# Stick-breaking attention on TensorE: the turns of the weight blocks made by the two row halves of the array, in pairs of key blocks, with the scores between both pairs

## The chip, the cores and the metric

One core of one Trainium2 chip runs the whole program. The metric is the device time of one execution in microseconds (us). All tensors are float32; the names ending in hi and lo are the two parts into which a float32 number is split for products in the fp32r format.

## The reference, cut to what matters

The layer has an input projection, an mLSTM branch, a stick-breaking attention branch and an output projection. The change lies in the attention branch alone: 8 heads of 64 features, 4096 tokens, strictly causal.

```python
def _stick_breaking(q, k, v):
    q = q.astype(f32) * (d ** -0.5)
    ...
        z = jnp.einsum('bthd,bshd->bhts', qb, kb)
        strict = jnp.arange(t1)[None, :] < jnp.arange(t0, t1)[:, None]
        log_beta = jax.nn.log_sigmoid(z)
        log_keep = jnp.where(strict, jax.nn.log_sigmoid(-z), 0.0)
        after = lax.cumsum(log_keep, axis=3, reverse=True) - log_keep
        A = jnp.where(strict, jnp.exp(log_beta + after), 0.0)
        outs.append(jnp.einsum('bhts,bshd->bthd', A, vb))
```

## The kernel before, in words

The program has three stages one after the other: `stage_project` (input projection), `stage_attend` (this one, from about 1576 to 3033 us of the profiled span) and `stage_mix` (mLSTM and output projection). The lines below are all of `stage_attend`.

The heads are taken in 4 pairs. For a pair, queries go in rows of 256 (two blocks of 128, index i), 16 rows per pair; a row walks backwards over the keys in chunks of 512. One row and one chunk are a *unit*: 288 units in all. 224 of them are full (two query blocks by 512 keys, two heads). The first unit of each of the 64 rows lies on the diagonal: in 32 of them the query blocks see 384 and 512 keys (long diagonal units), in the other 32 they see 128 and 256 (short ones).

What a unit does, engine by engine:

- TensorE, `scores` (L1316): q times k for two heads and two query blocks. The two heads sit in the two halves of the array's rows (64 features each) and write different PSUM banks (z, 4 banks). Three products of split parts each, so 12 matmuls of up to 512 columns.
- ScalarE, `gates` (L1398): keep = sigmoid(-z), four tiles of 128 queries by up to 512 keys, from PSUM into SBUF (8 tiles).
- GpSimd (L1292): on diagonal units only, the mask on the last keys.
- VectorE (L1467): four scans that multiply keep up along the keys from the back (`prod`, 3 units of buffer). In a full unit each scan begins with the last value of the same scan of the unit before.
- TensorE, `turn` (L1327): each 128 x 128 block of `prod` is transposed into PSUM (rt, 3 banks; a bank holds one key block of both heads and both query blocks). 16 transposes in a full unit, 14 in a long diagonal one, 6 in a short one; 4224 in all.
- ScalarE, `copies` (L1407): each rt bank is copied to SBUF (`turned`).
- TensorE, `weigh` (L1340): turned times the differences of the values (`dw`), into acc. 16 matmul instructions of 256 columns in a full unit, the two heads in the two halves of the array's columns.
- ScalarE, `row_out` (L1417): at the end of a row acc goes out.

The order is written out by hand, and each engine takes its own queue in order. TensorE does in iteration u: `turn(u)`, `scores(u + 2)`, `weigh(u - 1)`. ScalarE does `row_out(u - 2)`, `copies(u)`, `gates(u + 2)`. VectorE scans unit after unit. So the keep of a unit is made two units ahead. `turn(u)` waits until the four scans of unit u are done, and for each bank until the copy of three key blocks before has emptied it.

## Time and profile before

| | |
|---|---|
| time, median of 3 runs | 3558.57 us (3555.73 to 3559.9) |
| span of the profiled execution | 3554.5 us |
| busy over the whole span | PE 3472.8, PEld 2810.3, DVE 2494.5, ACT 1944.9, POOL 651.6 us |
| granted TensorE clock, mean | 0.989 |

The files name no device time of the profiled execution beside its span; of its own time only the span is known, and the median of the runs lies 4.1 us above it. PE stands for matmuls on TensorE, PEld for its weight loads (which run beside the matmuls), DVE for VectorE, ACT for ScalarE, POOL for GpSimd. A busy PE counts the time from a matmul's start to its modelled end, so it is near 100% wherever matmuls follow each other closely, whatever they deliver.

### The profile page before, as it was taken

To read this page: it belongs to the slowest core of one execution; us is meant where nothing else is said; L and a number is where in the kernel's file an instruction comes from. 1 tells how busy PE (TensorE), PEld (TensorE's weight loads), DVE (VectorE), ACT (ScalarE), POOL (GpSimd) and SP (SyncE) were. 2 spreads that over 40 slices of the span, in tenths; PEclk is the share of its full clock that TensorE was granted. 3 is DMA by queue.
4 is the path that set the end of the run, shared out by engine and by line. 5 is a ranking of instruction groups with operands and counts; after the bars stand their busy time and mean duration, and the time that the engine had idled before them with its cause. 6 is when DMAs were issued, how large, how long until landed. Compare 5 with 4: busy or idle time off the path is not lost. (4 is left out here: it accounts for less than half of the span.)

```text
span 3554.5 us, 66436 instructions
## 1 busy us (share of the span) xinstructions
PE 3472.8 (98%) x24178; PEld 2810.3 (79%) x24178; DVE 2494.5 (70%) x3501; ACT 1944.9 (55%) x4049; POOL 651.6 (18%) x677
## 2 busy tenths in 40 slices
PE   7998999999999999989999999999999999999998
PEld 4777888999999978867777777777777777788887
DVE  4664446334688862349898989899889989666665
ACT  4553223222444432237777777777777777555554
POOL 2312332100000024300103010300021002232332
PEclk8999999999999999989999999999999999999999
DMA  8989779877756689850012101210111001666663
GB/s 285 334 313 333 257 258 313 275 238 249 269 182 190 214 292 315 301 198 19 19 49 71 33 19 39 60 43 29 38 55 49 12 29 39 190 206 192 205 211 130
DMA packets 415584, 582.24 MB, mean 164 GB/s; under 512 B 35568, under 2 KB 298096, under 8 KB 414288
## 3 DMA queue, kind: packets, MB, share of 16 engines
q1 hardware_dynamic: 394560, 506.56, 43.3%
q0 software_dynamic: 16960, 58.73, 4.8%
q10 hardware_dynamic: 3792, 13.30, 1.0%
q8 instruction: 173, 2.83, 0.3%
q14 instruction: 99, 0.81, 0.1%
HBM read 393.74 MB, written 184.75 MB: 163 GB/s over the span
## 5 line engine op out<-in xcount | busy, mean ns | idle before, releaser
L1467 DVE TENSOR_TENSOR_SCAN a_prod<-a_keep,a_prod,a_zeros 128x512 f32<-128x512 f32 x896 | 1077.4, 1269 | 95.3 <-ACT a_keep L1398 92.9
L1407 ACT COPY a_turned<-a_rt 128x512 f32<-128x512 f32 x1088 | 547.2, 588 | 237.7 <-PE a_rt L1327 237.3
L1398 ACT ACTIVATE a_keep<-a_z 128x512 f32<-128x512 f32 (+3 forms) x1152 | 555.4, 572 | 41.2 <-PE a_z L1316 40.9
L1327 PEld LDWEIGHTS a_rt<-c_ident,a_prod 128*128 128x128 f32 x4224 | 452.7, 141 | 114.2 <-issue 56.1
L1327 PE MATMUL a_rt<-c_ident,a_prod 128*128 128x128 f32 x4224 | 532.3, 278 | 5.0 <-DVE a_prod L1467 3.7
L1340 PE MATMUL a_acc<-a_turned,c_dw 128*64 128x256 f32 x4352 | 519.6, 380 | 2.5 <-ACT a_osum L1417 2.5
L1340 PEld LDWEIGHTS a_acc<-a_turned,c_dw 128*64 128x64 f32 x4352 | 286.6, 136 | 214.7 <-issue 91.7
L1316 PE MATMUL a_z<-c_khi,a_q 64*128 64x512 f32 (+3 forms) x2304 | 372.8, 402 | 14.0 <-DMA c_dw<-scratch_dw 12.5
L939 DVE TENSOR_TENSOR p_hlo<-p_wraw,p_hlo 128x1024 fp32r<-128x1024 f32 x85 | 105.6, 1242 | 321.5 <-ACT p_hlo L704 321.5
L704 ACT CAST p_hlo<-p_wraw 128x1024 fp32r<-128x1024 f32 x85 | 89.1, 1049 | 391.5 <-PE p_bank L572 209.0
L1292 POOL TENSOR_SCALAR_AFFINE_SELECT a_keep<-a_keep 128x256 f32<-128x256 f32 x128 | 72.7, 571 | 1235.4 <-ACT a_keep L1398 1232.0
L1467 DVE TENSOR_TENSOR_SCAN a_prod<-a_keep,a_zeros 128x384 f32<-128x384 f32 (+3 forms) x256 | 228.8, 953 | 44.9 <-POOL a_keep L1292 44.9
L1316 PEld LDWEIGHTS a_z<-c_khi,a_q 64*128 64x128 f32 x2304 | 192.9, 186 | 82.7 <-issue 62.9
L1316 PE MATMUL a_z<-c_klo,a_q 64*128 64x512 f32 (+3 forms) x1152 | 219.0, 376 | 0.0
L939 DVE TENSOR_TENSOR p_aslot<-p_wraw,p_aslot 128x1024 fp32r<-128x1024 f32 x43 | 54.5, 1267 | 170.8 <-ACT p_aslot L704 170.8
L704 ACT CAST p_aslot<-p_wraw 128x1024 fp32r<-128x1024 f32 x43 | 45.1, 1048 | 203.4 <-PE p_bank L572 100.7
L640 POOL DMA_DIRECT2D p_hraw<-scratch_sbv x32 | 22.8, 717 | 710.7 <-DVE p_ob L1083 620.2
L572 PE MATMUL p_bank<-p_hhi,p_hlo 128*128 128x512 f32 x528 | 124.7, 394 | 5.7 <-DMA p_hlo<-scratch_parts 5.7
L572 PE MATMUL p_bank<-p_whi,p_hlo 128*128 128x512 f32 x528 | 125.3, 393 | 2.8 <-DMA p_hlo<-scratch_parts 2.8
L1316 PEld LDWEIGHTS a_z<-c_klo,a_q 64*128 64x128 f32 x1152 | 109.1, 185 | 21.2
L580 PE MATMUL p_bank<-p_hlo,p_whi 128*128 128x256 f32 x1008 | 124.5, 283 | 0.1
L580 PE MATMUL p_bank<-p_hlo,p_wlo 128*128 128x256 f32 x1008 | 124.4, 283 | 0.0
(297 smaller groups left out, 6257.3 us busy)
## 6 DMA issues: line engine op xcount, KB each, us to landing
p_hlo<-scratch_parts SPq DMA_DIRECT2D x130, 512.0 KB, 5.2
p_wraw<-scratch_sums SPq DMA_DIRECT2D x128, 512.0 KB, 6.7
p_aslot<-scratch_parts SPq DMA_DIRECT2D x62, 512.0 KB, 4.8
p_u<-in_w_in POOLq DMA_DIRECT2D x64, 256.0 KB, 5.8
scratch_wsums<-p_u POOLq DMA_DIRECT2D x32, 512.0 KB, 6.9
p_hraw<-scratch_sbv POOLq DMA_DIRECT2D x32, 512.0 KB, 7.3
m_xt<-in_x SPq DMA_DIRECT2D x32, 512.0 KB, 5.3
out_y<-c_pair SPq DMA_DIRECT2D x32, 512.0 KB, 4.6
```

What stands on the lines that cost most here:

```text
L572: last = pe.matmul(dst[:], stationary, moving, start=fresh and k == 0 and e == 0, stop=k == 3 and e == 2, skip_group_check=True)
L580: last = pe.matmul(part, stationary, moving, start=fresh and mm == 0 and k == 0 and e == 0, stop=k == 3 and e == 2, skip_group_check=True)
L640: pool.dma_start(t, out["sbv"][at:at + 2 * P, :].rearrange("(j p) d -> p j d", p=P)).then_inc((pre_in, zero_out)[e % 2], 16)
L704: act.copy(a_flat[q % 3][0], araw[k % 2]).then_inc(a_hi, 1)
L939: dve.tensor_tensor(al, araw[k % 2], ah.bitcast(F32), ALU.subtract).then_inc(a_lo, 1)
L1292: pool.affine_select(out=tail, in_=tail, compare_op=ALU.is_gt, fill=1.0, base=0, pattern=[[0, 2], [-1, P]], channel_multiplier=1).then_inc ...
L1316: mm = pe.matmul(z[(at + h) % ZB][:, 0:w], q_sb[e, g % 2, qp, t:t + P], k[e, s], start=part == 0, stop=part == 2)
L1327: last = pe.transpose(rt[k % RB][:, h * QW + i * P:h * QW + (i + 1) * P], prod[:, u % PB, 2 * i + h, kb * P:(kb + 1) * P], ident[:])
L1340: last = pe.matmul(acc[h * SD:(h + 1) * SD, lo:QW], dw[:, h, j * TPC + kb, :], turned[:, (FIRST[u] + kb) % TB, h * QW + lo:(h + 1) * QW], ...
L1398: act.activation(keep[:, at % KB, 0:w], z[at % ZB][:, 0:w], ACT.Sigmoid, scale=-Z_SCALE).then_inc(keep_done, 1)
L1407: act.copy(by_head(turned[:, k % TB]), by_head(rt[k % RB][:])).then_inc(turned_done, 1)
L1467: dve.tensor_tensor_scan(prod[:, u % PB, s, 0:w][:, ::-1], keep[:, at % KB, 0:w][:, ::-1], zeros[:, 0:w], first, ALU.mult, ALU.add).then_i ...
```

## The change

`turn` now handles a pair of key blocks. Each 128 x 128 transpose becomes two: queries 0 to 63 through the upper half of the array's rows and queries 64 to 127 through the lower half. Each has a stationary operand of 64 rows by 128 columns and a moving identity of 64 columns, and each half writes its own PSUM bank: a bank now holds 64 queries of every head and query block, for both key blocks of the pair. One semaphore step tells that a pair is turned. On ScalarE, `copies` handles a pair with one copy per bank (8 pieces of 64 columns, put back in order); a pair with a half-masked key block takes two smaller copies per bank. `turned` has 4 slots of a pair where it had 8 of a block (the same bytes). TensorE's order becomes `turn(u, 0)`, `scores(u + 2)`, `turn(u, 1)`, `weigh(u - 1)`, ScalarE's `row_out(u - 2)`, `copies(u, 0)`, `gates(u + 2)`, `copies(u, 1)`; short diagonal units have one pair only.

```diff
--- before.py
+++ after.py
@@ -1123,7 +1123,7 @@
                 UNITS.append((hp, row, cb, j))
     NU = len(UNITS)
     ZB, RB = 4, 3
-    KB, PB, TB = 8, 3, 8
+    KB, PB, TB = 8, 3, 4
     SPLIT_AT = ((), (0,), (1,), (2,), (3,), (4, 5), (6, 7), ())
     GATE_AT = ((), (0,), (1,), (2,), (3,), (), (), ())
 
@@ -1139,10 +1139,11 @@
     def skip(u, kb):
         return max(0, kb - UNITS[u][2] % 2 * 2) if diag(u) else 0
 
+    HB = P // 2
     FIRST, OWNER = [], []
     for u in range(NU):
         FIRST.append(len(OWNER))
-        OWNER += [u] * blocks(u)
+        OWNER += [u] * (blocks(u) // 2)
     FIRST.append(len(OWNER))
 
     with ExitStack() as ctx:
@@ -1153,7 +1154,7 @@
         khi, klo, dw, pair, ident, ones, maskb, xw, xs, bm = (held[k] for k in ("khi", "klo", "dw", "pair", "ident", "ones", "maskb", "xw", "xs", "bm"))
         keep = sb("keep", [P, KB, CH])
         prod = sb("prod", [P, PB, 4, CH])
-        turned = sb("turned", [P, TB, CH])
+        turned = sb("turned", [P, TB, 2, CH])
         zeros = sb("zeros", [P, CH])
         osum = sb("osum", [P, 2, QW])
         vrow, v_e = sb("vrow", [NT, SH * SD]), sb("v_e", [P, NP * NT])
@@ -1317,15 +1318,19 @@
                             if part == 2:
                                 mm.then_inc(z_done, 1)
 
-            def turn(u):
+            def turn(u, pair):
+                k = FIRST[u] + pair
                 pe.wait_ge(scan_done, 4 * u + 4)
-                for kb in range(blocks(u)):
-                    k = FIRST[u] + kb
-                    after(pe, turned_done, k + 1 - RB)
+                after(pe, turned_done, 2 * k + 2 - RB)
+                for b in range(2):
+                    kb = 2 * pair + b
                     for h in range(2):
                         for i in range(skip(u, kb), 2):
-                            last = pe.transpose(rt[k % RB][:, h * QW + i * P:h * QW + (i + 1) * P], prod[:, u % PB, 2 * i + h, kb * P:(kb + 1) * P], ident[:])
-                    last.then_inc(rt_done, 1)
+                            at = (4 * b + 2 * h + i) * HB
+                            for half in range(2):
+                                rows = slice(half * HB, (half + 1) * HB)
+                                last = pe.transpose(rt[(2 * k + half) % RB][:, at:at + HB], prod[rows, u % PB, 2 * i + h, kb * P:(kb + 1) * P], ident[rows, rows])
+                last.then_inc(rt_done, 1)
 
             def weigh(u):
                 _, row, cb, j = UNITS[u]
@@ -1333,11 +1338,11 @@
                     pe.wait_ge(g_act, 8)
                 if diag(u):
                     after(pe, row_done, row)
-                pe.wait_ge(turned_done, FIRST[u + 1])
+                pe.wait_ge(turned_done, 2 * FIRST[u + 1])
                 for kb in range(blocks(u)):
                     for h in range(2):
                         lo = skip(u, kb) * P
-                        last = pe.matmul(acc[h * SD:(h + 1) * SD, lo:QW], dw[:, h, j * TPC + kb, :], turned[:, (FIRST[u] + kb) % TB, h * QW + lo:(h + 1) * QW],
+                        last = pe.matmul(acc[h * SD:(h + 1) * SD, lo:QW], dw[:, h, j * TPC + kb, :], turned[:, (FIRST[u] + kb // 2) % TB, kb % 2, h * QW + lo:(h + 1) * QW],
                                          start=diag(u) and kb == 0, stop=j == 0 and kb == blocks(u) - 1, skip_group_check=True)
                 last.then_inc(av_done, 1)
 
@@ -1359,9 +1364,11 @@
             pe.matmul(acc[:, 2 * P:3 * P], ones[0:1, :], row(mlast_row), start=True, stop=True).then_inc(g_pe, 1)
             pe.wait_ge(g_act, 4)
             for u in range(NU):
-                turn(u)
+                turn(u, 0)
                 if u + 2 < NU:
                     scores(u + 2)
+                if blocks(u) > 2:
+                    turn(u, 1)
                 if u:
                     weigh(u - 1)
             weigh(NU - 1)
@@ -1397,14 +1404,19 @@
                     after(act, scan_done, at + 1 - KB)
                     act.activation(keep[:, at % KB, 0:w], z[at % ZB][:, 0:w], ACT.Sigmoid, scale=-Z_SCALE).then_inc(keep_done, 1)
 
-            def copies(u):
-                for kb in range(blocks(u)):
-                    k, lo = FIRST[u] + kb, skip(u, kb) * P
-                    act.wait_ge(rt_done, k + 1)
-                    if k >= TB:
-                        act.wait_ge(av_done, OWNER[k - TB] + 1)
-                    by_head = lambda t: t.rearrange("p (h q) -> p h q", h=2)[:, :, lo:] if lo else t
-                    act.copy(by_head(turned[:, k % TB]), by_head(rt[k % RB][:])).then_inc(turned_done, 1)
+            def copies(u, pair):
+                k, short = FIRST[u] + pair, skip(u, 2 * pair + 1)
+                act.wait_ge(rt_done, k + 1)
+                if k >= TB:
+                    act.wait_ge(av_done, OWNER[k - TB] + 1)
+                for half in range(2):
+                    src = rt[(2 * k + half) % RB][:].rearrange("p (s t) -> p s t", t=HB)
+                    dst = turned[:, k % TB].rearrange("p b (s e t) -> p (b s) e t", e=2, t=HB)[:, :, half]
+                    if short:
+                        act.copy(dst[:, 0:4], src[:, 0:4])
+                        act.copy(dst[:, 5:8:2], src[:, 5:8:2]).then_inc(turned_done, 1)
+                    else:
+                        act.copy(dst, src).then_inc(turned_done, 1)
 
             def row_out(u):
                 hp, row, cb, _ = UNITS[u]
@@ -1423,9 +1435,11 @@
             for u in range(NU):
                 if u >= 2:
                     row_out(u - 2)
-                copies(u)
+                copies(u, 0)
                 if u + 2 < NU:
                     gates(u + 2)
+                if blocks(u) > 2:
+                    copies(u, 1)
             row_out(NU - 2)
             row_out(NU - 1)
```

TensorE's queue in the middle of a row, before (a_rt is the PSUM tile of the turns, a_z that of the scores, a_acc that of the weighing):

```order
L1327 MATMUL a_rt<-c_ident,a_prod 128x128 x16
L1316 MATMUL a_z<-c_khi,a_q 128x512 x4
L1316 MATMUL a_z<-c_klo,a_q 128x512 x2
L1316 MATMUL a_z<-c_khi,a_q 128x512 x4
L1316 MATMUL a_z<-c_klo,a_q 128x512 x2
L1340 MATMUL a_acc<-a_turned,c_dw 64x256 x8
L1327 MATMUL a_rt<-c_ident,a_prod 128x128 x16
```

and the same place with the change:

```order
L1332 MATMUL a_rt<-c_ident,a_prod 128x64 x16
L1317 MATMUL a_z<-c_khi,a_q 128x512 x4
L1317 MATMUL a_z<-c_klo,a_q 128x512 x2
L1317 MATMUL a_z<-c_khi,a_q 128x512 x4
L1317 MATMUL a_z<-c_klo,a_q 128x512 x2
L1332 MATMUL a_rt<-c_ident,a_prod 128x64 x16
L1345 MATMUL a_acc<-a_turned,c_dw 64x256 x8
L1332 MATMUL a_rt<-c_ident,a_prod 128x64 x16
```

(The trace shows two instructions for each of the 8 products of the weighing, 16 in all.) The turns are cut in two parts of 16 with the scores between them, each with 64 columns where it had 128, and the scores no longer border on the weighing. The same place with the bank numbers, first before (one turn):

```order
L1327 MATMUL a_rt1<-c_ident,a_prod 128x128 [waits a_turned_done,a_scan_done]
L1327 MATMUL a_rt1<-c_ident,a_prod 128x128 x3
L1327 MATMUL a_rt2<-c_ident,a_prod 128x128 [waits a_turned_done]
L1327 MATMUL a_rt2<-c_ident,a_prod 128x128 x3
L1327 MATMUL a_rt0<-c_ident,a_prod 128x128 [waits a_turned_done]
L1327 MATMUL a_rt0<-c_ident,a_prod 128x128 x3
L1327 MATMUL a_rt1<-c_ident,a_prod 128x128 [waits a_turned_done]
L1327 MATMUL a_rt1<-c_ident,a_prod 128x128 x3
```

and with the change (the beginning of `turn(u, 0)`):

```order
L1332 MATMUL a_rt0<-c_ident,a_prod 128x64 [waits a_turned_done,a_scan_done]
L1332 MATMUL a_rt1<-c_ident,a_prod 128x64
L1332 MATMUL a_rt0<-c_ident,a_prod 128x64
L1332 MATMUL a_rt1<-c_ident,a_prod 128x64
L1332 MATMUL a_rt0<-c_ident,a_prod 128x64
L1332 MATMUL a_rt1<-c_ident,a_prod 128x64
```

Before, four transposes filled a bank and each bank was waited for by itself. Now neighbours go to two banks in turn, one row half each, and one wait stands ahead of all 16.

ScalarE's queue around one unit, before:

```order
L1407 COPY a_turned<-a_rt0 128x512 [waits a_av_done,a_rt_done]
L1407 COPY a_turned<-a_rt1 128x512 [waits a_av_done,a_rt_done]
L1407 COPY a_turned<-a_rt2 128x512 [waits a_av_done,a_rt_done]
L1407 COPY a_turned<-a_rt0 128x512 [waits a_av_done,a_rt_done]
L1398 ACTIVATE a_keep<-a_z0 128x512 [waits a_scan_done,a_z_done]
L1398 ACTIVATE a_keep<-a_z1 128x512 [waits a_scan_done,a_z_done]
L1398 ACTIVATE a_keep<-a_z2 128x512 [waits a_scan_done,a_z_done]
L1398 ACTIVATE a_keep<-a_z3 128x512 [waits a_scan_done,a_z_done]
L1407 COPY a_turned<-a_rt1 128x512 [waits a_av_done,a_rt_done]
```

and with the change:

```order
L1419 COPY a_turned<-a_rt2 128x8x64 [waits a_av_done,a_rt_done]
L1419 COPY a_turned<-a_rt0 128x8x64
L1405 ACTIVATE a_keep<-a_z0 128x512 [waits a_scan_done,a_z_done]
L1405 ACTIVATE a_keep<-a_z1 128x512 [waits a_scan_done,a_z_done]
L1405 ACTIVATE a_keep<-a_z2 128x512 [waits a_scan_done,a_z_done]
L1405 ACTIVATE a_keep<-a_z3 128x512 [waits a_scan_done,a_z_done]
L1419 COPY a_turned<-a_rt1 128x8x64 [waits a_av_done,a_rt_done]
L1419 COPY a_turned<-a_rt2 128x8x64
```

The four copies of a unit were together and waited each for its own bank; now two stand ahead of the four gates and two behind, and a wait stands only ahead of each pair.

## Rows read from the trace of the kernel before

**Rows 1.** Windows: busy us of each engine in two stretches.

```profile
core 0: us, PE busy (x) PEld busy (x) DVE busy (x) ACT busy (x) POOL busy (x), PEclk, DMA share, GB/s
1600.00:3020.00 1420.00, 1416.29 (x11830) 1011.95 (x11827) 1280.75 (x1132) 1112.73 (x2321) 201.94 (x247) 1.00 0.12 37
1577.80:1589.60 11.80, 9.68 (x44) 7.12 (x41) 10.04 (x18) 7.59 (x18) 3.47 (x5) 0.50 1.07 376
```

**Rows 2.** Timeline, PE, one iteration: start us, us, engine, what, count.

```profile
2376.19 1.99 PE L1327 MATMUL a_rt<-c_ident,a_prod 128*128 128x128 f32 x16
2378.11 0.73 PE L1316 MATMUL a_z<-c_khi,a_q 64*128 64x512 f32 x4
...
2379.69 1.95 PE L1340 MATMUL a_acc<-a_turned,c_dw 128*64 128x256 f32 x16
2381.57 1.99 PE L1327 MATMUL a_rt<-c_ident,a_prod 128*128 128x128 f32 x16
```

**Rows 3.** Timeline, DVE, scans; in brackets the idle time ahead and its releaser.

```profile
2183.42 2.06 DVE L1467 TENSOR_TENSOR_SCAN a_prod<-a_keep,a_zeros 128x128 f32<-128x128 f32 x4 [0.72 <-POOL a_keep L1292]
2187.96 19.17 DVE L1467 TENSOR_TENSOR_SCAN a_prod<-a_keep,a_prod,a_zeros 128x512 f32<-128x512 f32 x16 [2.48 <-ACT a_keep L1398]
...
2379.74 4.81 DVE L1467 TENSOR_TENSOR_SCAN a_prod<-a_keep,a_prod,a_zeros 128x512 f32<-128x512 f32 x4 [0.58 <-ACT a_keep L1398]
```

**Rows 4.** Costliest groups of the page: busy us, mean ns | idle before, releaser.

```profile
L1467 DVE TENSOR_TENSOR_SCAN a_prod<-a_keep,a_prod,a_zeros 128x512 f32<-128x512 f32 x896 | 1077.4, 1269 | 95.3 <-ACT a_keep L1398 92.9
...
L1327 PE MATMUL a_rt<-c_ident,a_prod 128*128 128x128 f32 x4224 | 532.3, 278 | 5.0 <-DVE a_prod L1467 3.7
...
L1467 DVE TENSOR_TENSOR_SCAN a_prod<-a_keep,a_zeros 128x384 f32<-128x384 f32 (+3 forms) x256 | 228.8, 953 | 44.9 <-POOL a_keep L1292 44.9
```

**Rows 5.** Waits, 1576 to 3040 us: total us, times, longest.

```profile
DVE a_prod L1467 <- ACT a_keep L1398: 92.9, 121, 2.5
...
DVE a_prod L1467 <- POOL a_keep L1292: 44.9, 60, 1.7
```

**Rows 6.** Timeline, ACT, one unit's copies and gates.

```profile
2376.88 2.05 ACT L1407 COPY a_turned<-a_rt 128x512 f32<-128x512 f32 x4 [1.10 <-PE a_rt L1327]
2379.11 2.06 ACT L1398 ACTIVATE a_keep<-a_z 128x512 f32<-128x512 f32 x4 [0.17 <-PE a_z L1316]
```

**Rows 7.** Timeline, transposes at full clock: ten matmuls in a row.

```profile
2209.15 1.26 PE L1327 MATMUL a_rt<-c_ident,a_prod 128*128 128x128 f32 x10
```

**Rows 8.** Timeline, weight loads of transposes at half clock: L1327's.

```profile
1586.89 2.58 PEld L1327 LDWEIGHTS a_rt<-c_ident,a_prod 128*128 128x128 f32 x12
...
1589.24 0.23 PEld L1327 LDWEIGHTS a_rt<-c_ident,a_prod 128*128 128x128 f32 x1
```

**Rows 9.** Timeline, weight loads of L1348's transposes (32 moving columns) at half clock.

```profile
1578.66 0.43 PEld L1348 LDWEIGHTS a_rt<-c_ident,a_vrow 32*128 32x128 f32 x3
...
1578.88 0.22 PEld L1348 LDWEIGHTS a_rt<-c_ident,a_vrow 32*128 32x128 f32 x1
```

**Rows 10.** Timeline, PEld, scores of a short diagonal unit, both row halves.

```profile
2226.74 0.19 PEld L1316 LDWEIGHTS a_z<-c_khi,a_q 64*128 64x128 f32 x2
2226.85 0.19 PEld L1316 LDWEIGHTS a_z<-c_klo,a_q 64*128 64x128 f32 x2
```

**Rows 11.** Timeline, PE, the matmuls of the same scores.

```profile
2226.63 0.44 PE L1316 MATMUL a_z<-c_khi,a_q 64*128 64x128 f32 x4
...
2227.02 0.45 PE L1316 MATMUL a_z<-c_khi,a_q 64*128 64x256 f32 x4
```

**Rows 12.** Timeline, PE and PEld, from the last transpose to the scores.

```profile
2210.70 0.27 PE L1327 MATMUL a_rt<-c_ident,a_prod 128*128 128x128 f32 x1
...
2210.90 0.30 PEld L1316 LDWEIGHTS a_z<-c_khi,a_q 64*128 64x128 f32 x4 [0.17 <-issue]
```

**Rows 13.** Timeline, PE in `stage_mix`, transposes then matmuls of one shape.

```profile
3201.87 0.60 PE L1607 MATMUL mp_t<-c_ident,c_khi 128*128 128x128 f32 x4
3202.30 0.50 PE L1611 MATMUL mp_s<-c_khi 128*128 128x128 f32 x3
```

## The prediction

> **What bounds the kernel now.** I first read the windows over the attention stage [rows 1]. In its 1420 us PE counts as busy for 1416, DVE for 1281, ACT for 1113, and the granted clock is 1.00. PE's busy time says little by itself, since it runs to each matmul's modelled end, so I went to the timeline. One iteration with full units goes from one turn's start to the next: 2376.19 to 2381.57, 5.38 us [rows 2]. In it the turn takes 1.92, the scores 1.58, the weighing 1.88, and no idle time stands ahead of any. The scans of the same iteration take 4.81, with 0.58 idle ahead until ACT's keep comes, which waits for the scores [rows 3]; copies and gates take 2.05 and 2.06 [rows 6]. So PE is the bound in the middle of a row, DVE is second, 0.6 us behind, and ACT third, at some 4.1. The groups and the waits say the same of the whole stage: the scans are busy for 1077.4 + 228.8 = 1306.2 us and idle for 95.3 + 44.9 = 140.2 ahead of them [rows 4], in 121 + 60 waits [rows 5]. Whatever PE gains can at most take DVE's waits away.
>
> **The pace of a turn.** At full clock ten transposes span 1.26 us, the last of them about 0.27 long [rows 7, 4]: (1.26 - 0.27) / 9 = 0.11 us each. What sets this, the 128 moving columns or the 128 columns of the weight load? At half clock (0.50 [rows 1]) it is (1589.24 - 1586.89) / 11 = 0.214 [rows 8]: it follows the clock. In the same slow stretch the small transposes with 32 moving columns have weight loads of 128 columns as well, and two such loads are (1578.88 - 1578.66) / 2 = 0.11 apart [rows 9]. So the load of a transpose needs at most 0.11 at half clock, hence about 0.055 at full clock, while 128 moving columns need 0.214 and 0.11. The moving side is the bound, and the change halves it: 64 columns in 0.055, beside a load of 0.055.
>
> **Do both halves run side by side?** The scores already work so: two loads of 64 rows by 128 columns start together and the next two start 0.11 later [rows 10], one pair in the time of one ordinary load. I therefore take 0.056 us for a pair of half transposes where a whole one took 0.11. 16 pairs in a full unit: 0.90 in place of 1.75, a gain of 0.85. The bounds: 0.055 from below (both the loads and the columns need it), and from above two halves in series, each at 0.11 as now, 0.22 a pair. I take the lower end because rows 9 and rows 10 are each the nearest kind (a transpose's load; two row halves).
>
> **The changes of shape.** From turn to scores the array goes from 128 rows to 64. The last transpose starts at 2210.70, the next would at 2210.81, but the scores' weights start at 2210.90 and their second pair 0.11 later [rows 12] (four loads in 0.30, each 0.19), which is when the first weights are in. So the change costs 0.09 + 0.11 = 0.20 us. Afterwards turns and scores have one shape (64 rows by 128 columns). From transposes to ordinary matmuls of one shape there is no gap: four transposes from 3201.87 at 0.11 end at 3202.30, where the next matmul starts [rows 13]. So 0.20 goes away in each unit; if it stayed, I would lose it. The weighing's own two borders remain, now with turns on both sides. PE's iteration becomes 5.38 - 0.85 - 0.20 = 4.33 us, below DVE's 4.8.
>
> **What DVE then takes.** Sixteen scans back to back span 19.17 us, 4.79 a unit [rows 3]. PE's 4.33 leaves 0.45. The order does not make a new wait in the middle of a row. Count from the end of unit u's scans, T. The first pair is turned at about T + 0.8 (0.06 to start, 0.45, and 0.27 for the last to come out). ACT copies until T + 1.8 (half of 2.05 for two). The first scores are in PSUM near T + 1.6, the gates run from T + 1.8 to 3.8 [rows 6]; DVE wants them at T + 4.8. The second pair is turned at T + 2.6 and copied from 3.8 to 4.8; its first copy, at 4.3, frees the bank that the next turn needs at 4.8. Behind `turn(u, 1)` on PE waits only the weighing, which uses copies of the unit before. The smaller copies of diagonal units are new: at most two more per bank, some 0.4 us each unit, in ACT's spare 0.7; without that cover they would cost 64 x 0.4 = 26 us.
>
> Waits that stay: behind each of the 32 short diagonal units. Its scans take 2.06, or 1.98 without the last one's latency; the next unit's first keep is ready at T + 2.4 (1.8 and a gate's 0.6), and where that unit now makes DVE idle for 2.48 [rows 3] it will be some 0.45. 32 times that is 14 us. At the three borders of head pairs the single-unit rows and the masks follow each other closely: some 2 us each, 6. The first units run at half clock [rows 1]: 6. Sum 26. Against that, 181 waits fall away nearly all, and with each the latency of a last scan that the next now covers: 4.81 for four gives (4.81 - 1.27) / 3 = 1.18 a scan against 1.27 alone, so 0.08 x 181 = 14 us.
>
> **The sum**, on the profiled execution: DVE's stage was 1306 + 140 = 1446; it becomes 1306 - 14 + 26 = 1318. That is 128 us less: a span of 3554.5 - 128 = 3426.5, and with the 4.1 us by which the median of the runs lies above the span, **3431 us**. The floor with no wait of DVE at all is 3558.6 - 140 - 14 = 3405. The sum doesn't hang on the 0.056: PE stays under DVE's 4.79 as long as a pair takes less than 0.109 - (5.18 - 4.79) / 16 = 0.084.
>
> **The rivals.**
>
> *The turns gain nothing, only the borders do.* If a load of 64 rows doesn't have the quick form of rows 9 but the one of rows 10 (0.11), a pair takes 0.11 again. PE's iteration is 5.18; 288 x 0.20 = 58 us less, 3501. For it: rows 10 are the only 64-row loads. Against: those are not transposes. Chance 0.09.
>
> *The issue of instructions becomes the bound: slower.* The change doubles the matmuls of a turn to 32. The densest stretch that I find has six matmuls from 2226.63 to 2227.02, 0.065 each [rows 11]. If that were a price per matmul, a pair takes 0.13, PE's iteration 5.18 + 16 x 0.021 = 5.52, and the time 3558.6 + 288 x 0.14 = 3599. It decides from a pair of 0.109 + 0.20 / 16 = 0.122 on. Against: those six are held by their loads, 0.11 a pair. Chance 0.06.
> The Trainium skill (TensorE: Matmul & The Clock Gate, "Wait — 56ns, not 53.3ns?") has a rule of this kind: with hardware decode off, microcode spends about 62 ns on a matmul, else no start follows another in under some 25 ns. By the first a pair would take 0.124, an estimate of 3570 us; by the second 0.05, and the sum stands. No row here decides between them. Its page TensorEngine Tiling (Array Packing), "Instruction Overhead", also warns against taking the factor from a dimension that is already small, for about 60 cycles go with each matmul; 64 columns stand right at that.
>
> *The halves run one after the other: much slower.* A pair takes 0.22, PE's iteration 5.18 + 1.76 = 6.94, 288 x 1.56 = 449 us more, 4008. Against: rows 10. Chance 0.04.
>
> *The stage gains half.* A pair takes near 0.095, or the strided copies take half as long again (ACT 5.1 of 4.8): 3460 to 3490. Chance 0.06.
>
> *The forecast*, 3405 to 3450: 0.73. The remaining 0.02 is a measured time within 0.2% of before (about what a measurement of this kernel can tell from no change), where gains and issue cost cancel.
>
> **How the numbers follow.** Faster: 0.73 + 0.06 + 0.09 = 0.88, less 0.02 for a borders-only case in which even the borders stay: 0.86. Of that 0.02, half is no change and half slower: same 0.02 + 0.01 = 0.03, slower 0.06 + 0.04 + 0.01 = 0.11. The range reaches from the floor, 3405, to just past the borders-only case, 3505.
>
> **What would show it.** Right: starts of pairs of half transposes 0.056 apart, and scores' weights loading during the last of them, with no gap; an iteration of 4.8 us with DVE's scans in long unbroken runs, and PE's turn now waiting for the scans; DVE's idle time down from 140 to some 26 us. Wrong: pairs 0.11 or more apart (then PE is still the bound and DVE idles as before), the gap of 0.20 between turn and scores still there, ACT's copies much above their 0.6, or a granted clock below 1.00 in the stage once PE has time to wait.

## The result and the profile after

The changed kernel takes 3420.7 us (median of 4 runs, 3420.18 to 3421.55), beside 3558.65 for the kernel before on the same chip (4 runs, 3555.73 to 3559.9): a ratio of 0.9613, interval 0.9602 to 0.9624. That is 138 us less. The forecast was 3431, 128 less. The profiled execution took 3420.38 us with a span of 3418.6, so the span fell by 3554.5 - 3418.6 = 135.9. The granted clock is 0.99 over the span, as before.

First the costliest groups of the page after, those that answer to [rows 4], and the masks of GpSimd.

```profile
L1481 DVE TENSOR_TENSOR_SCAN a_prod<-a_keep,a_prod,a_zeros 128x512 f32<-128x512 f32 x896 | 1067.7, 1265 | 3.0 <-ACT a_keep L1405 1.8
...
L1332 PE MATMUL a_rt<-c_ident,a_prod 64*128 64x64 f32 x8448 | 369.0, 226 | 94.8 <-DVE a_prod L1481 62.3
...
L1481 DVE TENSOR_TENSOR_SCAN a_prod<-a_keep,a_zeros 128x384 f32<-128x384 f32 (+3 forms) x256 | 234.5, 974 | 6.4 <-POOL a_keep L1293 6.4
```

DVE's idle time ahead of the scans was 140.2 and is 3.0 + 6.4 = 9.4. With their busy time the scans hold DVE for 1067.7 + 234.5 + 9.4 = 1311.6 us, where it was 1446.4 [rows 4]: 134.8 less, nearly the whole 135.9. So the time came out of DVE's waits, and PE now waits for DVE. The windows over the stage show the same turn of roles beside [rows 1]: PE is busy for 93% and DVE for 99%, at full clock.

```profile
core 0: us, PE busy (x) PEld busy (x) DVE busy (x) ACT busy (x) POOL busy (x), PEclk, DMA share, GB/s
1600.00:2880.00 1280.00, 1190.63 (x15968) 873.47 (x15966) 1271.61 (x1131) 1093.17 (x2442) 251.64 (x245) 1.00 0.14 41
```

The timeline of PE in the change, one iteration in the middle of a row, answers to [rows 2].

```profile
2253.13 0.71 PE L1332 MATMUL a_rt<-c_ident,a_prod 64*128 64x64 f32 x16 [0.17 <-DVE a_prod L1481]
2253.65 0.71 PE L1317 MATMUL a_z<-c_khi,a_q 64*128 64x512 f32 x4
...
2255.12 0.66 PE L1332 MATMUL a_rt<-c_ident,a_prod 64*128 64x64 f32 x16
2255.71 1.95 PE L1345 MATMUL a_acc<-a_turned,c_dw 128*64 128x256 f32 x16
2257.83 0.71 PE L1332 MATMUL a_rt<-c_ident,a_prod 64*128 64x64 f32 x16 [0.17 <-DVE a_prod L1481]
```

From turn to turn it is 2257.83 - 2253.13 = 4.70 us, where it was 5.38. The two parts of the turn take 0.52 and 0.59 to the next group's start, the scores 1.47. The weighing has 2.12 until the next turn, of which it needs 1.88 [rows 2]; the other 0.24 is the wait for the scans. PE's own work is thus 0.52 + 1.47 + 0.59 + 1.88 = 4.46.

The timeline of DVE in the change answers to [rows 3].

```profile
2196.37 2.43 DVE L1481 TENSOR_TENSOR_SCAN a_prod<-a_keep,a_zeros 128x128 f32<-128x128 f32 x4
2198.87 9.76 DVE L1481 TENSOR_TENSOR_SCAN a_prod<-a_keep,a_prod,a_zeros 128x512 f32<-128x512 f32 x8
2208.87 5.44 DVE L1481 TENSOR_TENSOR_SCAN a_prod<-a_keep,a_zeros 128x384 f32<-128x384 f32 x4 [0.24 <-POOL a_keep L1293]
...
2234.77 4.20 DVE L1481 TENSOR_TENSOR_SCAN a_prod<-a_keep,a_zeros 128x384 f32<-128x384 f32 x4 [0.93 <-POOL a_keep L1293]
2238.89 23.59 DVE L1481 TENSOR_TENSOR_SCAN a_prod<-a_keep,a_prod,a_zeros 128x512 f32<-128x512 f32 x20
```

Twenty scans in one run span 23.59; less the last one's 1.265 and over 19 that is 1.175 each, 4.70 a unit, which is PE's iteration. Behind the short diagonal unit of 2196.37 the next scan starts at 2198.87 with no idle time. Two long diagonal units of the same shape take 4.20 and 5.44, which the experiments with GpSimd take up.

The waits of the change from 1576 to 2900 us (total us, times, longest):

```profile
PEld a_rt L1332 <- DVE a_prod L1481: 175.2, 219, 2.7
...
PE a_rt L1332 <- DVE a_prod L1481: 62.3, 122, 2.5
...
PE a_rt L1332 <- ACT a_turned L1419: 24.7, 29, 1.0
```

The turn's weights and matmuls wait for the scans in most units. The 29 waits for ACT's copies are nearly all at the turn that follows a short diagonal unit's weighing (0.93 us ahead of the turn at 2209.02). The kernel before had no such waits; they cost next to nothing here, since the chained scans idle for only 3.0 us in all.

### The profile page after: what moved, and what is told of

The parts are those of the page before. It is cut to its first block and busy times, and to the rows that moved or that the text cites. A ratio compares the mean times of both kernels' runs of the same rounds, so it can differ in the third digit from the quotient of the medians.

```text
span 3418.6 us, 74728 instructions
## 1 busy us (share of the span) xinstructions
PE 3246.3 (95%) x28402; PEld 2670.1 (78%) x28402; DVE 2486.0 (73%) x3501; ACT 1925.7 (56%) x4177; POOL 705.0 (21%) x677
## 3 DMA queue, kind: packets, MB, share of 16 engines
q1 hardware_dynamic: 394560, 506.56, 44.9%
## 5 line engine op out<-in xcount | busy, mean ns | idle before, releaser
L1481 DVE TENSOR_TENSOR_SCAN a_prod<-a_keep,a_prod,a_zeros 128x512 f32<-128x512 f32 x896 | 1067.7, 1265 | 3.0 <-ACT a_keep L1405 1.8
L1419 ACT COPY a_turned<-a_rt 128x512 f32<-128x512 f32 x960 | 529.8, 622 | 170.4 <-PE a_rt L1332 169.9
L1332 PEld LDWEIGHTS a_rt<-c_ident,a_prod 64*128 64x128 f32 x8448 | 328.4, 139 | 236.5 <-DVE a_prod L1481 175.2
L1332 PE MATMUL a_rt<-c_ident,a_prod 64*128 64x64 f32 x8448 | 369.0, 226 | 94.8 <-DVE a_prod L1481 62.3
L1293 POOL TENSOR_SCALAR_AFFINE_SELECT a_keep<-a_keep 128x256 f32<-128x256 f32 x128 | 128.6, 1017 | 1045.5 <-ACT a_keep L1405 1045.0
L1481 DVE TENSOR_TENSOR_SCAN a_prod<-a_keep,a_zeros 128x384 f32<-128x384 f32 (+3 forms) x256 | 234.5, 974 | 6.4 <-POOL a_keep L1293 6.4
L1317 PEld LDWEIGHTS a_z<-c_khi,a_q 64*128 64x128 f32 x2304 | 199.8, 189 | 32.8 <-issue 14.8
```

The source lines that it names most:

```text
L1293: pool.affine_select(out=tail, in_=tail, compare_op=ALU.is_gt, fill=1.0, base=0, pattern=[[0, 2], [-1, P]], channel_multiplier=1).then_inc ...
L1317: mm = pe.matmul(z[(at + h) % ZB][:, 0:w], q_sb[e, g % 2, qp, t:t + P], k[e, s], start=part == 0, stop=part == 2)
L1332: last = pe.transpose(rt[(2 * k + half) % RB][:, at:at + HB], prod[rows, u % PB, 2 * i + h, kb * P:(kb + 1) * P], ident[rows, rows])
L1419: act.copy(dst, src).then_inc(turned_done, 1)
L1481: dve.tensor_tensor_scan(prod[:, u % PB, s, 0:w][:, ::-1], keep[:, at % KB, 0:w][:, ::-1], zeros[:, 0:w], first, ALU.mult, ALU.add).then_i ...
```

## The experiments

The theory under test: halving the moving columns takes PE below DVE, the order with the scores between the two parts is needed for that, and from there on DVE alone sets the pace. Line numbers beyond an edit are shifted by the lines that it adds. Each ratio is to the kernel before as measured beside that experiment: 3558.55 us for 1 to 4, 3556.93 for 5 to 7, 3558.24 for 8 to 10. Differences of a few us between experiments are therefore not told apart by the times alone.

**1. The halves without the new order.**

```diff
                 turn(u, 0)
-                if u + 2 < NU:
-                    scores(u + 2)
                 if blocks(u) > 2:
                     turn(u, 1)
+                if u + 2 < NU:
+                    scores(u + 2)
...
                 copies(u, 0)
-                if u + 2 < NU:
-                    gates(u + 2)
                 if blocks(u) > 2:
                     copies(u, 1)
+                if u + 2 < NU:
+                    gates(u + 2)
```

> The row halves as in the change, but both pairs of a unit are turned one after the other ahead of the scores (and copied one after the other ahead of the gates). Theory (the scores between the pairs hide the copy that empties the one bank the second pair lacks): the second pair waits for the last transpose to come out (0.27 us) and one copy (0.65), some 0.9 us in each full unit, PE's iteration goes from 4.4 to about 5.3 us and the time to 3540 us (3500 to 3580). Rival (the place of the scores is worth nothing, the pace of the halves gives all): 3421 us, with no wait of a turn for a copy.

Measured: 3574.39 us (5 runs, 3567.78 to 3581.99), ratio 1.0043, interval 1.0023 to 1.0064. That is within the range and 34 us above the value expected: the whole gain is gone. The timeline of its PE:

```profile
2249.77 0.71 PE L1332 MATMUL a_rt<-c_ident,a_prod 64*128 64x64 f32 x16
2251.29 0.71 PE L1332 MATMUL a_rt<-c_ident,a_prod 64*128 64x64 f32 x16 [0.81 <-ACT a_turned L1419]
```

And its waits from 1576 to 3040 us:

```profile
PE a_rt L1332 <- ACT a_turned L1419: 173.5, 224, 0.9
DVE a_prod L1481 <- ACT a_keep L1405: 96.5, 118, 2.3
DVE a_prod L1481 <- POOL a_keep L1293: 60.0, 63, 2.5
```

A unit needs four banks at two a pair and there are three, so the second part waits 0.81 us for the first copy, with nothing behind it on PE that could run. PE's iteration in the middle of a row is 5.46 us (turns at 2255.09 and 2260.55 in the same trace) where it was 5.38, and 224 x 0.08 = 18. DVE idles for 96.5 + 60.0 = 156.5 in these waits, where it was 92.9 + 44.9 = 137.8 [rows 5]: 19 more, and the time is 16 more.

**2. The new order without the halves.** Before's `turn` and `copies` with whole transposes, each cut after two key blocks (shown for `turn`; `copies` is cut and ordered in the same way):

```diff
-            def turn(u):
+            def turn(u, pair):
                 pe.wait_ge(scan_done, 4 * u + 4)
-                for kb in range(blocks(u)):
+                for kb in (2 * pair, 2 * pair + 1):
...
-                turn(u)
+                turn(u, 0)
                 if u + 2 < NU:
                     scores(u + 2)
+                if blocks(u) > 2:
+                    turn(u, 1)
```

> The kernel before (whole 128 x 128 transposes, a copy per key block) with the order of the change alone: two key blocks turned, scores, two key blocks turned, weighing. Theory (the halves side by side give the gain, the order alone gives none): turns keep their 0.11 us each and there are more changes of shape, about 0.2 us more per full unit: 3605 us (3580 to 3630). Rival (the finer interleaving gives the gain): under 3500 us.

Measured: 3589.14 us (2 runs), ratio 1.0078, interval 1.0049 to 1.0107. Its PE:

```profile
2251.26 1.09 PE L1327 MATMUL a_rt<-c_ident,a_prod 128*128 128x128 f32 x8
2252.29 0.73 PE L1316 MATMUL a_z<-c_khi,a_q 64*128 64x512 f32 x4
...
2253.87 1.09 PE L1327 MATMUL a_rt<-c_ident,a_prod 128*128 128x128 f32 x8
2254.89 0.87 PE L1340 MATMUL a_acc<-a_turned,c_dw 128*64 128x256 f32 x8
```

Eight transposes now hold PE for 1.03 and 1.02 until the next group, 2.05 in place of 1.92 [rows 2], while the scores take 2253.87 - 2252.29 = 1.58 as before. The additional 0.13 is the change of shape that now stands behind each of the two parts; 224 x 0.13 = 29 of the 31 us. With experiment 1 this closes a square: 3558.6 with neither, 3574 with the halves alone, 3589 with the order alone, 3421 with both. Each part alone costs; neither of them holds the gain.

**3. The halves issued in series.** Of each pair of key blocks all upper row halves first, then all lower ones.

```diff
-                for b in range(2):
-                    kb = 2 * pair + b
-                    for h in range(2):
-                        for i in range(skip(u, kb), 2):
-                            at = (4 * b + 2 * h + i) * HB
-                            for half in range(2):
-                                rows = slice(half * HB, (half + 1) * HB)
+                for half in range(2):
+                    rows = slice(half * HB, (half + 1) * HB)
+                    for b in range(2):
+                        kb = 2 * pair + b
+                        for h in range(2):
+                            for i in range(skip(u, kb), 2):
+                                at = (4 * b + 2 * h + i) * HB
```

> The change, but in each pair all transposes of the upper row half are issued first and then all of the lower, so that neighbours share a row half. Theory (the gain in pace is that the two halves run side by side): each half transpose now takes the 0.063 us that a pair took, a full unit's turns 2.0 us in place of 1.0, PE's iteration 5.4 us, and the time is 3570 us (3530 to 3600). Rival (half-size transposes are cheap whatever stands beside them, or the queue pairs them up by itself): 3421 us.

Measured: 3457.09 us (2 runs), ratio 0.9707, interval 0.9679 to 0.9735. The expectation was wrong by 113 us. The timeline of its PE shows why:

```profile
2199.91 0.83 PE L1332 MATMUL a_rt<-c_ident,a_prod 64*128 64x64 f32 x13
2200.52 0.49 PE L1317 MATMUL a_z<-c_khi,a_q 64*128 64x512 f32 x1
2200.58 0.35 PE L1332 MATMUL a_rt<-c_ident,a_prod 64*128 64x64 f32 x3
2200.74 0.70 PE L1317 MATMUL a_z<-c_khi,a_q 64*128 64x512 f32 x3
```

Three transposes of the lower half start from 2200.58 on, behind a scores' matmul at 2200.52 that is issued after them. The upper half was through with its eight and went on to its part of the scores, while the lower half, which had begun later, caught up. So this order of issue does not put the halves in series: each row half goes through its own matmuls in order, whatever the other has still to do. What is lost is the uneven ends, as an iteration in the middle of a row shows:

```profile
1704.75 0.80 PE L1332 MATMUL a_rt<-c_ident,a_prod 64*128 64x64 f32 x13 [0.85 <-ACT a_turned L1419]
...
1706.84 0.96 PE L1332 MATMUL a_rt<-c_ident,a_prod 64*128 64x64 f32 x16
1707.73 1.95 PE L1345 MATMUL a_acc<-a_turned,c_dw 128*64 128x256 f32 x16
1709.61 0.82 PE L1332 MATMUL a_rt<-c_ident,a_prod 64*128 64x64 f32 x13
```

The second part holds PE for 0.89 until the weighing, where it is 0.59 in the change, and the iteration is 1709.61 - 1704.75 = 4.86 with no idle time in it. That is 0.16 above DVE's 4.70, and 224 x 0.16 = 36 us: PE is just the bound again. The lag shows at the diagonal units. DVE idles for 26.0 + 23.4 = 49.4 us in the page of this kernel, 40 more than in the change, and the time is 36 more.

**4 and 5. How much room PE has.** All turns twice, and then only the first block of the second part twice, 8 half transposes more in a full unit:

```diff
-                for b in range(2):
+                for b in (0, 0, 1, 1):
```

```diff
-                for b in range(2):
+                for b in ((0, 1), (0, 0, 1))[pair]:
```

> The change with each half transpose issued twice (the same values written again). Theory (after the change DVE is the bound at 4.8 us a full unit and PE at 4.4 has 0.4 in hand): 1.0 us more on PE per full unit, of which 0.4 is hidden: iteration 5.4 us, time 3580 us (3550 to 3610). Rival (PE is still the bound of the changed kernel): all of it is paid, 3421 + 264 x 1.0 = 3690 us.

> The change with one key block in four of each full unit turned twice (8 half transposes more, 0.25 us of PE). Theory (DVE is the bound at 4.79 us a full unit, PE's own work is 4.47): PE's work becomes 4.72, nearly all of it is hidden: 3421 to 3432 us. Rival (PE is still the bound): 224 x 0.25 = 56 us more, 3477 us.

Measured: 3594.85 us (2 runs), ratio 1.0094, interval 1.0065 to 1.0123; and 3423.92 us (4 runs), ratio 0.963, interval 0.9616 to 0.9645. Doubled turns cost 174 us; a quarter more costs 3 (6 by the ratios, whose intervals overlap). In the page of the kernel with doubled turns the groups of the scans show DVE waiting again, 174.1 us:

```profile
L1481 DVE TENSOR_TENSOR_SCAN a_prod<-a_keep,a_prod,a_zeros 128x512 f32<-128x512 f32 x896 | 1078.5, 1269 | 111.3 <-ACT a_keep L1405 111.2
...
L1481 DVE TENSOR_TENSOR_SCAN a_prod<-a_keep,a_zeros 128x384 f32<-128x384 f32 (+3 forms) x256 | 228.9, 953 | 62.8 <-POOL a_keep L1293 62.8
```

With a quarter more, the timeline of PE is:

```profile
2254.29 0.71 PE L1332 MATMUL a_rt<-c_ident,a_prod 64*128 64x64 f32 x16
...
2256.29 0.90 PE L1332 MATMUL a_rt<-c_ident,a_prod 64*128 64x64 f32 x24
2257.12 1.95 PE L1345 MATMUL a_acc<-a_turned,c_dw 128*64 128x256 f32 x16
2259.00 0.71 PE L1332 MATMUL a_rt<-c_ident,a_prod 64*128 64x64 f32 x16
```

The iteration is 4.71 us with no idle time on PE at all: the added turns took 0.83 - 0.59 = 0.24, just the wait that PE had in the change. PE and DVE stand level there. Beyond that point PE's time counts: the other 24 half transposes of a full unit bring 171 us. With doubled turns PE's iteration is 5.46 (turns at 2245.73 and 2251.19 in that trace), 0.76 above DVE's 4.70, and 224 x 0.76 = 170.

**6 and 8. Work added on DVE.** In each unit from the ninth on (280 of 288), a memset of 128 by 128, or a scan over 128 columns, into a buffer that is free in this stage:

```diff
             for u in range(NU):
+                if u >= 8:
+                    dve.memset((soft, fg, ig, u_g)[u % 4][:], 0.0)
```

```diff
             for u in range(NU):
+                if u >= 8:
+                    dve.tensor_tensor_scan((soft, fg, ig, u_g)[u % 4][:], zeros[:, 0:P], zeros[:, 0:P], 0.0, ALU.mult, ALU.add)
```

> The change with one more DVE instruction in each unit from the ninth on: a memset of 128 x 128 into a tile that nobody reads by then. Theory (DVE is the bound, its scans stand back to back): the time grows by 280 times what the memset takes from its start to the next scan's start, which I put at 0.1 us: 28 us more, 3449 us (3435 to 3470). Rival (DVE has slack): within 5 us of 3421.

> As the memset experiment, but the extra DVE instruction of each unit from the ninth on is a scan of 128 columns (0.39 us alone, 0.34 from start to start), which the memset of 0.07 to 0.09 us was too short to stand for: that memset's place was mostly given back, since the scan behind it began 0.10 us sooner than behind a scan. Theory (DVE is the bound): 280 times 0.24 to 0.34 us more, 3421 + 80 = 3500 us (3485 to 3520). Rival (DVE has slack of its own): under 3440 us.

Measured: the memset 3425.7 us (4 runs), ratio 0.9635, interval 0.962 to 0.965; the scan 3502.04 us (4 runs), ratio 0.9843, interval 0.9828 to 0.9858. The memset missed its expectation: it costs 5 us in all (8 by the ratios). The timeline of its DVE:

```profile
1662.00 4.68 DVE L1483 TENSOR_TENSOR_SCAN a_prod<-a_keep,a_prod,a_zeros 128x512 f32<-128x512 f32 x4
1666.66 0.17 DVE L1471 MEMSET a_u<- 128x128 f32 x1
1666.75 4.68 DVE L1483 TENSOR_TENSOR_SCAN a_prod<-a_keep,a_prod,a_zeros 128x512 f32<-128x512 f32 x4
```

A unit takes 1666.75 - 1662.00 = 4.75, 0.05 more than the change's 4.70, though the memset is 0.17 long and takes 0.09 until the next start: four scans and a memset don't cost the sum. Over the 224 full units 0.05 makes 11 us; from the first scan's start to the last one's end this trace has 1312.9 us where the change has 1304.4, 8.5 more, since some waits get shorter. The four span 4.68; less two steps of 1.175 and the last one's 1.25, the first step is 1.08. So a scan behind a memset hands over 0.09 earlier than one behind a scan. That made the memset the wrong test for DVE as the bound. The scan is the right one: 81 us over 280 units is 0.29 us each, the length to be expected of it, and it shows in full. In the page of that kernel no wait is left ahead of the chained scans, and 3.5 us ahead of the others:

```profile
L1483 DVE TENSOR_TENSOR_SCAN a_prod<-a_keep,a_prod,a_zeros 128x512 f32<-128x512 f32 x896 | 1080.1, 1267 | 0.0
...
L1483 DVE TENSOR_TENSOR_SCAN a_prod<-a_keep,a_zeros 128x384 f32<-128x384 f32 (+3 forms) x256 | 228.8, 951 | 3.5 <-POOL a_keep L1293 3.5
```

**7, 9 and 10. GpSimd beside the diagonal scans.** With DVE as the bound, its own slow places count. A group of the page of before stands against the same of the change:

```profile
L1292 POOL TENSOR_SCALAR_AFFINE_SELECT a_keep<-a_keep 128x256 f32<-128x256 f32 x128 | 72.7, 571 | 1235.4 <-ACT a_keep L1398 1232.0
```

```profile
L1293 POOL TENSOR_SCALAR_AFFINE_SELECT a_keep<-a_keep 128x256 f32<-128x256 f32 x128 | 128.6, 1017 | 1045.5 <-ACT a_keep L1405 1045.0
```

A mask took 571 ns and takes 1017. Where it used to fall beside DVE's waits, it now falls beside a scan, and the diagonal scans rose too, from 228.8 [rows 4] to 234.5. The timeline of GpSimd in the change shows more of its work (the w_out split and the gate sums) beside the unit of 5.44 us at 2208.87:

```profile
2209.17 1.38 POOL L1263 TENSOR_TENSOR c_wout_lo<-c_pair,c_wout_hi 128x256 fp32r<-128x256 f32 x1
2210.51 1.57 POOL L1282 TENSOR_SCALAR a_wpart<-c_pair,c_csil 128x256 f32<-128x256 f32 x1
2212.16 1.07 POOL L1284 TENSOR_TENSOR c_gate_sum<-c_gate_sum,a_wpart 128x256 f32<-128x256 f32 x1
```

Experiment 7 leaves GpSimd only the first unit's masks. In the other diagonal units four small matmuls per query block add a large negative number to the masked scores, and DVE waits for the keep itself and not for GpSimd; at -1024 some masked places stay partly open, so this part of the computation differs. Experiment 9 instead holds the split and the gate sums back until the unit's scans are done. Experiment 10 does both, with -65536. The edits of 7 and 9 follow; of 7 the loading of `pick` and `far` and DVE's new wait are left out.

```diff
                     pool.wait_ge(keep_done, 4 * u + 2 * i + 2)
+                    if u:
+                        continue
...
+                        if part == 1 and diag(u) and u:
+                            pe.wait_ge(g_in, 48 + 128)
+                            for half in range(2):
+                                for h in range(2):
+                                    e = slice(h * SD, (h + 1) * SD)
+                                    pe.matmul(z[(at + h) % ZB][:, w - P:w], pick[half][e], far[half][e], start=False, stop=False, skip_group_check=True)
```

```diff
                 k, r = UNITS[u][1] // 8, UNITS[u][1] % 8
+                if SPLIT_AT[r]:
+                    pool.wait_ge(scan_done, 4 * u + 4)
```

> The change, and the mask of every diagonal unit but the first made by PE and not by GpSimd: four matmuls of 64 rows per query block add -1024 to the masked scores, so that keep comes out as 1 there. DVE's diagonal scans then neither wait for GpSimd nor run beside its masks. Theory (DVE is the bound, and its diagonal scans are slowed while GpSimd masks: 47 us above their own fastest in sum, 62 with all scans): 25 to 45 us less, 3385 us (3375 to 3400), with the diagonal scans' mean near 0.85 us where it is 0.974. Rivals: the slow scans have another cause (the means stay, 3415 us), or the mask's 64 x 0.9 us of PE work isn't hidden (3430 us and more).

> The change, with GpSimd's work for the output weights held back until the four scans of the diagonal unit are done, so that it runs beside chained scans and not beside diagonal ones; the masks stay on GpSimd. In the change, first scans beside GpSimd's instructions take 1555 ns where they take 1192 alone (512 columns), chained ones 1333 where they take 1254. Theory (what GpSimd runs beside the diagonal scans slows them, and DVE is the bound): 15 to 35 us less, 3396 us (3385 to 3408). Rival (the slow scans are only moved to the chained ones): 3421 us.

> Both: GpSimd's work for the output weights held back as above, and the masks of all diagonal units but the first made by PE, with -65536 in place of -1024 (scores here are large, so -1024 did not close every masked place). Theory: no diagonal scan runs beside GpSimd, the 60 us by which diagonal scans exceed their own fastest go nearly all, PE's work for the masks is hidden: 3380 us (3368 to 3392). Rival (the mask on PE adds as much as it saves once DVE's scans are short): 3396 us or more.

Measured: 3413.3 us (5 runs), ratio 0.9597, interval 0.9584 to 0.9611; 3423.45 us (5 runs), ratio 0.962, interval 0.9607 to 0.9633; 3417.19 us (5 runs), ratio 0.9604, interval 0.959 to 0.9617. All three intervals overlap the change's 0.9602 to 0.9624, so none is clearly better, and the 20 to 40 us that I had hoped for are not there. The scans' groups in the pages of 7, 9 and 10, in this order:

```profile
L1502 DVE TENSOR_TENSOR_SCAN a_prod<-a_keep,a_prod,a_zeros 128x512 f32<-128x512 f32 x896 | 1060.5, 1261 | 12.1 <-ACT a_keep L1424 11.4
L1502 DVE TENSOR_TENSOR_SCAN a_prod<-a_keep,a_zeros 128x384 f32<-128x384 f32 (+3 forms) x256 | 224.8, 939 | 5.1 <-ACT a_keep L1424 4.1
```

```profile
L1483 DVE TENSOR_TENSOR_SCAN a_prod<-a_keep,a_prod,a_zeros 128x512 f32<-128x512 f32 x896 | 1095.9, 1297 | 11.5 <-ACT a_keep L1407 11.1
...
L1483 DVE TENSOR_TENSOR_SCAN a_prod<-a_keep,a_zeros 128x384 f32<-128x384 f32 (+3 forms) x256 | 199.6, 839 | 9.5 <-POOL a_keep L1293 9.5
```

```profile
L1504 DVE TENSOR_TENSOR_SCAN a_prod<-a_keep,a_prod,a_zeros 128x512 f32<-128x512 f32 x896 | 1088.5, 1290 | 23.8 <-ACT a_keep L1426 23.8
...
L1504 DVE TENSOR_TENSOR_SCAN a_prod<-a_keep,a_zeros 128x384 f32<-128x384 f32 (+3 forms) x256 | 190.9, 808 | 3.7 <-ACT a_keep L1426 2.9
```

With GpSimd's other work held back, the diagonal scans fall by 34.9 us and the chained ones rise by 28.2: the slowness goes where GpSimd's work goes. In 10 the scans are busy for 22.8 us less than in the change, but idle for 23.8 + 3.7 = 27.5, 18.1 more: with its scans faster, a short diagonal unit is done before the next unit's keep is there (23.8 us of waits for ACT). Busy and idle together are 1316.5 in 9 and 1306.9 in 10, beside the change's 1311.6; in 7 they are 1302.5, and its 7 us are about that.

## Why the prediction was right

*What bounds what.* PE was the bound and DVE the second, 0.6 us behind, as read from [rows 2, 3]. The change turned this round: PE's wait for the scans in the profile after, experiment 5 (PE level at 4.71) and experiments 4 and 8 (full price beyond) show it from both sides.

*The pace of a pair.* The step said 0.056; a pair takes 0.063. The timeline of the change's PE has it at a turn:

```profile
2204.92 0.60 PE L1332 MATMUL a_rt<-c_ident,a_prod 64*128 64x64 f32 x14
```

Seven pairs in 0.60, less the last one's 0.22, over six: 0.063. The same comes from experiment 5, 0.24 for four pairs more. So the lower bound was nearly met and the halves do run side by side. That is under the 0.084 up to which the sum was said to hold, and so 16 x 0.007 = 0.11 us of PE cost nothing. (With DVE's 4.70 and PE's wait of 0.24 the limit is 0.063 + 0.24 / 16 = 0.078.) Whether the 64 moving columns or the load of 128 columns sets the 0.063 no run tells apart; the prediction put both at 0.055. One matmul thus takes 0.031 of issue at most, and the rival of a bound in the issue (0.13 a pair) is out. The 62 ns for each matmul that the Trainium skill names for hardware decode off (TensorE: Matmul & The Clock Gate, "Wait — 56ns, not 53.3ns?") is not what this kernel meets, and the 0.05 a pair by its other rule, some 25 ns from start to start, was nearer.

*The changes of shape.* The border of 0.20 between turn and scores was said to go. It did: the scores start 0.52 behind the first of eight pairs, 8 x 0.063 + 0.02. Experiment 2, which has more of these borders, pays 31 us. PE's iteration came to 4.46 where the sum had 4.33: 0.11 from the pair, 0.02 here.

*DVE's unit.* The step took 4.79 from one run of sixteen scans; the run of twenty gives 4.70. GpSimd did nothing beside those sixteen, as its timeline of before has it:

```profile
2207.52 0.41 POOL L1292 TENSOR_SCALAR_AFFINE_SELECT a_keep<-a_keep 128x256 f32<-128x256 f32 x1 [23.48 <-ACT a_keep L1398]
```

The 4.79 counts the last scan's full length, 0.09 over the four units, and short waits inside the run that the timeline doesn't print: the eighth and the ninth scan start 1.40 apart and not 1.175. It left the sum as it was, since that went by the busy total: 1306 - 14 = 1292 was said, and it is 1302.2. The 14 for latency do come, but the masks and GpSimd's other work now lie beside scans and take 10 back. That term was missing.

*The waits that stay* were put at 26 us and are 9.4. The term that came out otherwise is the 14 behind the short diagonal units. The next unit was to start 1.98 + 0.45 = 2.43 behind one's start, and in the row it starts 2198.87 - 2196.37 = 2.50 behind it, with no idle time: the short unit's scans, beside GpSimd's work, take 2.43 where I used 1.98, and fill the wait. In experiment 9, which moves most of that work away from them, the chained scans wait 11.5 us, near the 14. So the 10 of busy time too many and most of the idle time that is missing are one thing, and that they cancel in part is luck. The borders and first units, 12 in the sum, are most of the 9.4. Of the 10 us between forecast and result, the two errors in DVE's terms, +10 busy and -17 idle, make 7; 2 more lie around the span, where the median is 2.1 us above the span and the sum added 4.1.

*The order of the work* was costed at no new wait. Experiment 1 shows how much hung on that: 154 us lie between the two orders of the same instructions. The prediction followed the banks through one unit and found the copy in time; it did not say that the halves alone would be slower, nor that the order was half of the change.

*The halves in series*, the rival of 4008, took 0.22 a pair. Experiment 3 shows that its price was wrong as well as its case: three transposes of one half, 0.35 less the last one's 0.22 over two, are 0.065 apart, not 0.11, and the two halves don't wait for each other. The Trainium skill (TensorEngine Tiling (Array Packing), "Key Properties") states that different tiles load and multiply in parallel; the rows of experiment 3 agree.

## What to carry to other kernels

Where loads and matmuls of the two row halves run side by side, halving the moving columns of small transposes takes their time from 0.109 to 0.063 here, though it doubles their count and their banks; if the banks no longer suffice for all of them, put other work between the parts, or the wait for the copies takes the whole gain (3574 against 3421). Here that work has the same array shape; with another shape on each side, experiment 2 pays 0.13 us a unit. Work out first which engine is next and how far behind it is: 0.6 us a unit was all that could be had, and a pair up to 0.078 would have given nearly the same time (experiment 5 adds as much work and costs 3 us). Beyond that, what PE's iteration has above DVE's 4.70, times the 224 full units, is the cost: 36 us of the 36 in experiment 3, 170 of the 174 in experiment 4. To test whether an engine is the bound, add the same kind of work that it does; a cheap odd instruction can hide in a latency.

## What the runs showed of the hardware that I had not expected

- Each row half of the array keeps its own order. A matmul of the upper half (scores, 2200.52) starts before transposes of the lower half that are issued ahead of it (2200.58). The order of issue between halves cost 36 us in place of the expected 149.
- A memset of 0.17 us between scans costs DVE 0.05 a full unit, 5 us of the whole time in place of 28: the scan behind it hands over in 1.08 where one behind a scan takes 1.175.
- DVE's scans and GpSimd's elementwise work slow each other: a long diagonal unit takes 4.20 with only a mask of 0.62 us beside it and 5.44 beside more of GpSimd's work, a mask 571 and 1017 ns. Moving GpSimd's work moved the slowness from one group of scans to the other (-34.9, +28.2) and didn't remove it. What the two share was not told apart.
